# Three up projections of a fused transformer kernel: two-product wide form with halves added by VectorE, and a fourth low part made by GpSimd

## The reference, cut to what matters

```python
xt = x.reshape(T, D)                       # T = 256 tokens, D = 2048
q = (xt @ w_pq).reshape(T, PEER_HEADS, 2, PEER_HALF)
...                                        # top 16 of 128 x 128 keys for each of 8 heads, softmax gates
# the kernel computes, for all experts e in four quarters of 32 blocks of 128:
#   hid[e, t]  = gelu(u_emb[e] . x[t])           "up"
#   hid[e, t] *= gate[e, t]                      (gates spread from the chosen slots)
#   y[t]      += hid[e, t] * v_emb[e]            "down"
```

## Time and profile before

| what | value |
|---|---|
| time, median of 3 runs | 3218.45 us (3217.82 to 3219.81) |
| profiled execution | 3219.95 us, of it 3218.3 us span |
| PE busy | 3172.9 us, 99% |
| DVE busy | 2416.1 us, 75% |
| ACT busy | 1592.2 us, 49% |
| POOL busy | 644.3 us, 20% |
| chain that ended last | PE 88%, DVE 5%, issue 3%, ACT 2% |
| 256-column products of `block_product` | 3 lines x 2944 |
| low parts by DVE (L1985), mean | 872 x 1223 ns |
| low parts by POOL (L488), mean | 160 x 2439 ns |
| load of an `ada` tile, issue to landing | 4.6 us |

### The profile page before, as it was taken

One profiled execution on the slowest core, in us unless ns is written; L12 is line 12 of the kernel. 1 busy time (PEld: TensorE's weight loads), 2 busy tenths in 40 slices (PEclk: granted clock), 3 DMA queues, 4 the chain that ended last, 5 costly groups with the idle time before them and its releaser, 6 DMA issues.

```text
span 3218.3 us, 61750 instructions
## 1 busy us (share of the span) xinstructions
PE 3172.9 (99%) x20344; PEld 2833.6 (88%) x20344; DVE 2416.1 (75%) x3958; ACT 1592.2 (49%) x2291; POOL 644.3 (20%) x635
## 2 busy tenths in 40 slices
PE   8999999999999999999999999999999999999997
PEld 8898899999889998899878888888998888888886
DVE  6676577699778987799999776445899878655556
ACT  5764545433443345433444457655766444444443
POOL 1050058100111011100000115887221111100000
PEclk9999999999999999999999999999999999999999
DMA  6436555666887678866655884666776887866444
GB/s 214 147 109 190 182 165 182 194 212 213 255 265 219 213 222 258 267 198 213 200 179 175 269 265 146 189 191 205 243 235 206 293 274 232 257 194 190 146 137 157
DMA packets 185936, 667.80 MB, mean 208 GB/s; under 512 B 24192, under 2 KB 24416, under 8 KB 184528
## 3 DMA queue, kind: packets, MB, share of 16 engines
q1 hardware_dynamic: 149984, 545.91, 53.6%
q0 software_dynamic: 35824, 120.19, 12.2%
HBM read 663.82 MB, written 2.18 MB: 207 GB/s over the span
## 4 chain that ended last, share of the span: by engine, by line
PE 88%; DVE 5%; issue 3%; ACT 2%; POOL 1%; DMA 0%; DVEq 0%; ACTq 0%; POOLq 0%; SPq 0%
PE PS L577 11%; PE PS L579 11%; PE PS L578 11%; PE PS L591 8%; PE PS L1008 7%; PE PS L1010 7%; PE PS L1012 7%; PE PS L592 4%; PE PS L720 2%; PE PS L722 2%; PE PS L721 2%; PE PS L1194 2%; PE PS L1196 2%; PE PS L1198 2%; POOL w_lo L488 1%
## 5 line engine op out<-in xcount | busy, mean ns | idle before, releaser
L1372 ACT ACTIVATE w_hi<-raw 128x1024 fp32r<-128x1024 f32 x1032 | 1091.8, 1059 | 1330.5 <-PE PS L579 579.0
L1985 DVE TENSOR_TENSOR w_lo<-raw,w_hi 128x1024 fp32r<-128x1024 f32 x872 | 1065.5, 1223 | 501.5 <-ACT w_hi L1372 494.8
L577 PE MATMUL PS<-xt,w_hi 128*128 128x256 f32 x2944 | 849.5, 289 | 2.3 <-DVEq L2118 2.1
L578 PE MATMUL PS<-xt,w_hi 128*128 128x256 f32 x2944 | 833.3, 283 | 0.0
L579 PE MATMUL PS<-xt,w_lo 128*128 128x256 f32 x2944 | 833.1, 283 | 0.0
L577 PEld LDWEIGHTS PS<-xt,w_hi 128*128 128x128 f32 x2944 | 564.4, 192 | 10.9 <-issue 9.6
L591 PE MATMUL PS<-xt,w_hi 128*128 128x512 f32 x1560 | 563.9, 403 | 7.6 <-DVE xt L2040 4.2
L578 PEld LDWEIGHTS PS<-xt,w_hi 128*128 128x128 f32 x2944 | 565.0, 192 | 0.4
L579 PEld LDWEIGHTS PS<-xt,w_lo 128*128 128x128 f32 x2944 | 564.7, 192 | 0.0
L488 POOL TENSOR_TENSOR w_lo<-raw,w_hi 128x1024 fp32r<-128x1024 f32 x160 | 387.5, 2439 | 350.2 <-ACT w_hi L1372 222.4
L592 PE MATMUL PS<-xt,w_lo 128*128 128x256 f32 x1560 | 438.7, 281 | 0.0
(11 more groups left out here) (445 smaller groups left out, 4029.1 us busy)
## 6 DMA issues: line engine op xcount, KB each, us to landing
raw<-in_u_emb SPq DMA_DIRECT2D x256, 512.0 KB, 3.6
raw<-in_v_emb SPq DMA_DIRECT2D x256, 512.0 KB, 4.4
ada<-in_ada_w POOLq DMA_DIRECT2D x240, 256.0 KB, 4.6
raw<-in_xbc SPq DMA_DIRECT2D x96, 512.0 KB, 3.5
raw<-in_z SPq DMA_DIRECT2D x80, 512.0 KB, 3.6
raw<-in_q SPq DMA_DIRECT2D x64, 512.0 KB, 3.5
raw<-in_a_out SPq DMA_DIRECT2D x64, 512.0 KB, 4.3
raw<-in_k SPq DMA_DIRECT2D x48, 512.0 KB, 4.8
```

Source lines behind the costliest of these rows:

```text
L577: pe.matmul(o, w_h, x_h, start=start, stop=False, skip_group_check=True)
L578: pe.matmul(o, w_h, x_l, start=False, stop=False, skip_group_check=True)
L1372: act.activation(w_hi[:, u, :], raw[:, u, :], ACT.Copy).then_inc(hi_done, 1)
L1985: dve.tensor_tensor(w_lo[:, u, :], raw[:, u, :], w_hi[:, u, :].bitcast(F32), ALU.subtract)\
```

## The change

In up1, up2 and up3 a block is made by `wide_block`. ScalarE copies the second half of the bank to `second_half` (the buffer `xtmp`), VectorE adds both halves into `hid` (`halves_summed`), and ScalarE applies Gelu in place in `hid`. A block on TensorE waits for `halves_added` (the sum two blocks before) and not for the Gelu, but for the first body. In the loop GpSimd makes the low part of tile 3 of each body, after the three of VectorE; VectorE waits at the top of each body until all four of the body before are there.

```diff
-        WIDE = {"w_pq": 0, "xbc": 16, "k2": 64, "q2": 88}
+        WIDE = {"w_pq": 0, "up1": 16, "up2": 48, "up3": 80, "xbc": 112, "k2": 160, "q2": 184}
...
             for quarter in range(1, QUARTERS):
-                with pool.Fori(0, 16) as k:
+                f = FIRST_BODY[f"up{quarter}"]
+                with pool.Fori(0, 15) as k:
                     for slot, segment in enumerate((0, 5)):
                         ada_tile(f"up{quarter}", segment, k, quarter - 1, slot, ada)
+                    pool.wait_ge(lo_done, 4 * (k + (f + 1)) + 3)
+                    low(k + (f + 1), 3)
...
                         spread_parts(2 * j + b, n_before, b, 2 + 2 * b)
-                        pe.wait_ge(act_free, 2 * j + (ACT_BLOCKS[up] + b + 1))
-                        block_product(up, j, b, PS[:, b, 0:S])
+                        if type(j) is int:
+                            pe.wait_ge(act_free, ACT_BLOCKS[up] + b + 1)
+                        else:
+                            pe.wait_ge(sem("halves_added"), 2 * j + (WIDE[up] + b + 1))
+                        wide_block(up, j, b)
...
+                def half(i, b, body):
                     act.wait_ge(tile_used, 4 * body + 2 * b + 2)
-                    act.activation(one(hid[quarter % 2], i), PS[:, b, 0:S], ACT.Gelu_apprx_tanh).then_inc(act_free, 1)
+                    half_out(up, i, b).then_inc(sem("half_out"), 1)
+
+                def gelu(i):
+                    act.wait_ge(sem("halves_added"), i + (WIDE[up] + 3))
+                    act.activation(one(hid[quarter % 2], i), one(hid[quarter % 2], i), ACT.Gelu_apprx_tanh)\
+                        .then_inc(act_free, 1)
+
+                def body(j):
+                    high(j + (f + 1), 0)
+                    if type(j) is not int:
+                        gelu(2 * j - 1)
+                    high(j + (f + 1), 1)
+                    half(2 * j, 0, j + f)
+                    high(j + (f + 1), 2)
+                    gelu(2 * j)
+                    high(j + (f + 1), 3)
+                    half(2 * j + 1, 1, j + f)
...
                 for u in range(4):
                     stage_hid(quarter - 1, u, u)
+                gelu(30)
                 high(f + 16, 2)
                 high(f + 16, 3)
-                gelu(31, 1, f + 15)
+                half(31, 1, f + 15)
+                gelu(31)
...
+                def halves_summed(i, b):
+                    dve.wait_ge(sem("half_out"), i + (WIDE[up] + 1))
+                    dve.tensor_tensor(one(hid[quarter % 2], i), PS[:, b, 0:S], second_half[:, b, :], ALU.add)\
+                        .then_inc(sem("halves_added"), 1)
 
                 def body(j):
+                    dve.wait_ge(lo_done, 4 * (j + (f + 1)))
                     for u in range(4):
-                        low(j + (f + 1), u)
+                        if u < 3:
+                            low(j + (f + 1), u)
                         if u % 2 == 0:
                             key_rows(2 * j + (2 + u // 2), n_before, (quarter - 1) * EB, u // 2)
                             apply_parts(2 * j + u // 2, n_before, quarter - 1, u // 2, 2 + u // 2 * 2)
                         else:
                             ada_product(f"up{quarter}", j, u // 2, ada, acc_up)
+                            halves_summed(2 * j + u // 2, u // 2)
...
                 low(f + 16, 1)
+                halves_summed(30, 0)
                 dve.wait_ge(sem("gates_applied"), 2 + EB * quarter)
                 for u in range(4):
                     stage_hid(quarter - 1, u, u, u)
...
                 low(f + 16, 2)
                 low(f + 16, 3)
+                halves_summed(31, 1)
```

More of the change, by code:

```diff
@@ L519, in _ @@
             for quarter in range(1, QUARTERS):
-                with pool.Fori(0, 16) as k:
+                f = FIRST_BODY[f"up{quarter}"]
+                with pool.Fori(0, 15) as k:
                     for slot, segment in enumerate((0, 5)):
                         ada_tile(f"up{quarter}", segment, k, quarter - 1, slot, ada)
+                    pool.wait_ge(lo_done, 4 * (k + (f + 1)) + 3)
+                    low(k + (f + 1), 3)
+                for slot, segment in enumerate((0, 5)):
+                    ada_tile(f"up{quarter}", segment, 15, quarter - 1, slot, ada)
                 down = f"down{quarter - 1 if quarter < 3 else 3}"
@@ L1686, in up_stage @@
                 f = FIRST_BODY[f"up{quarter}"]
-                def gelu(i, b, body):
+                up = f"up{quarter}"
+                def half(i, b, body):
                     act.wait_ge(tile_used, 4 * body + 2 * b + 2)
-                    act.activation(one(hid[quarter % 2], i), PS[:, b, 0:S], ACT.Gelu_apprx_tanh).then_inc(act_free, 1)
[L1692 to L1698, removed]
+                    half_out(up, i, b).then_inc(sem("half_out"), 1)
[13 more added lines that the diff above has]
+                    half(2 * j + 1, 1, j + f)
+                body(0)
+                with act.Fori(1, 15) as j:
+                    body(j)
                 high(f + 16, 0)
+                gelu(29)
                 high(f + 16, 1)
-                gelu(30, 0, f + 15)
+                half(30, 0, f + 15)
                 act.wait_ge(sem("gates_applied"), 2 + EB * quarter)
@@ L2462, in up_stage @@
                 down = f"down{quarter - 1}"
+                up = f"up{quarter}"
                 link(dve.memset(acc_up[:, :, :], 0.0))
+                if quarter > 1:
+                    dve.wait_ge(stage_lo_done, CHUNKS[f"down{quarter - 2}"] + 2 * EB)
+                def halves_summed(i, b):
+                    dve.wait_ge(sem("half_out"), i + (WIDE[up] + 1))
+                    dve.tensor_tensor(one(hid[quarter % 2], i), PS[:, b, 0:S], second_half[:, b, :], ALU.add)\
+                        .then_inc(sem("halves_added"), 1)
                 def body(j):
+                    dve.wait_ge(lo_done, 4 * (j + (f + 1)))
                     for u in range(4):
-                        low(j + (f + 1), u)
+                        if u < 3:
+                            low(j + (f + 1), u)
                         if u % 2 == 0:
@@ L2480, in up_stage @@
                     body(j)
+                dve.wait_ge(lo_done, 4 * (f + 16))
                 low(f + 16, 0)
```

## The result

| | before | after |
|---|---|---|
| time, median of 20 runs | 3217.75 us (3215.25 to 3222.06) | 3226.89 us (3222.59 to 3230.74) |
| profiled execution | 3219.95 us, span 3218.3 | 3226.84 us, span 3224.9 |
| DVE busy | 2416.1 us | 2439.0 us |
| POOL busy | 644.3 us | 758.0 us |

The ratio is 1.0026, 95% interval 1.002 to 1.0032: slower by 9 us. I had forecast slower, but by 59 us: 3278, with a range from 3236.

What follows compares the result with a forecast made beforehand. TensorE bounds the kernel, with VectorE nearly full; the change makes VectorE the bound. Loops +50.9 and tails +8.5 sum to +59.4 us: 3279.4 against its own execution, forecast as 3278, range 3236 to 3302.

Steps and rivals of the forecast that it cites:

- Step 1, TensorE's products: Up loops: two wide products instead of three narrow save 0.095 us a block, 9.2 us at most; TensorE needs 12.16 a body.
- Step 2, VectorE's steps: Up loops: one low part leaves, two sums of halves come; VectorE's own steps fill 11.36 us a body, below TensorE's 12.16.
- Step 3, the stall: Up loops: GpSimd's low part locks out VectorE's `hot_gate`, 2.15 us a body; body 13.51 us, loops together +50.9 us.
- S + 7.9: Up loop body: GpSimd asks about 7.9 us after VectorE's body start S, during `hot`, and gets in behind it.
- rival A (the short stall): Up loops: GpSimd starts only with the sum of gates, `hid` waits 1.2 us; body 12.6, 3238 us; chance 0.16.
- Step 4, the tails: Ends of up1 to up3: VectorE's tail precedes the last Gelu; +1.9, +1.9 and +4.7 us, together +8.5.
- rival D: Up loops: TensorE's idle of 1.3 us a body halves its clock for microseconds in many bodies; +20, 3299 us; chance 0.06.

Runs made afterwards that it cites:

- runs 13 and 14: After with narrow last blocks and the last Gelu ahead of ScalarE's last high part: with GpSimd's low part 3209.08 us, without it 3207.57 us.
- run 7: After plus an extra VectorE write of 128 x 256 in each loop body: 3279.16 us.
- Runs 6 and 8: After plus a 128x512 VectorE write a body: without GpSimd's low part 3247.48 us; with it waiting for the last `hot_gate` 3269.06 us.
- Run 4: After plus products that nobody reads in TensorE's waits for the last Gelu at the stage ends: 3221.46 us.
- run 3: After with the last block of each up stage in the narrow form, Gelu straight from `PS`: 3211.16 us.
- run 11: After plus two VectorE writes (128 x 768 and 128 x 512) once per stage, behind the third body: 3234.65 us.
- run 12: After plus an extra VectorE write of 128 x 64 in each loop body: 3258.23 us.
- run 5: After plus an extra VectorE write of 128 x 512 in each loop body, GpSimd's low part kept: 3294.07 us.
- run 2: The kernel before, narrow products kept, with only GpSimd making each body's fourth low part: 3218.86 us.
- run 9: After plus one VectorE write of 128 x 768 per stage behind the third body, GpSimd's low part kept: 3228.54 us.

## Why the prediction was wrong

The term that failed is VectorE's own steps, 11.36 us a body where 11.09 were measured. With it fell the conclusion that VectorE comes late and loses 2.15 us a body to GpSimd: it lost 1.1 us, and TensorE stayed the bound.

**Step 1, TensorE's products: right.** The body that TensorE can do is 12.18 us (I had 12.16), and without the tails the whole gain shows (runs 13 and 14).

**Step 2, VectorE's steps: the term that was mis-sized.** I had 11.36 us, it is 11.09. I took 0.74 for `ada_product` from a distance of 1.05 us less 0.31 of waiting, but an instruction that waits loses its overlap with the one before: from start to start it is 0.66 (641.47 to 642.13), and 0.08 twice a body is most of the error. The prediction's own tail had it right: 1.32 for two, from a stretch in which VectorE didn't wait. The sum of halves is 0.33 and not 0.38, which is another 0.10 for two.

**Step 3, the stall: the lock was right, but GpSimd came in at another place.** 11.09 + 1.1 us is just TensorE's 12.18, so VectorE stays nearly on time. ScalarE's high part of tile 3 then follows TensorE, and GpSimd asks at S + 8.6 (638.87 - 630.28), late in the three `hot_gate`, instead of S + 7.9. In run 7, as in the prediction, it follows the Gelu and with it VectorE's halves (ScalarE's timelines, after and then run 7):

```profile
637.72 1.06 ACT L1380 ACTIVATE w_hi<-raw 128x1024 fp32r<-128x1024 f32 x1 [0.71 <-PE PS L599]
```
```profile
650.08 0.42 ACT L1705 ACTIVATE hid<-hid  x1 [1.96 <-DVE hid L2496]
650.40 1.04 ACT L1381 ACTIVATE w_hi<-raw 128x1024 fp32r<-128x1024 f32 x1
```

Run 7 puts 0.20 of the missing 0.27 us back, and the long stall comes, with 3279 us. Runs 6 and 8 show that it isn't the write as such: the larger write costs 20 us without GpSimd, and with GpSimd moved the long stall stays away. So 0.20 us in a body of 12 were worth some 52 us in the whole. I had given rival A (the short stall) a body of 12.6 us, from the same 11.36; with the right steps its mechanism is what happened, but the body stays at TensorE's pace.

After itself is near that edge. VectorE is slower than TensorE by 0.01 to 0.02 us a body: from the second body of up1 to the last the request slips from 0.55 to 0.32 us behind the first `hot_gate`, in up3 to 0.24, and GpSimd still comes in behind all three each time.

The Trainium skill (SBUF — State Buffer, section Who interferes with whom) says that whoever issues first gets the pair for the whole instruction. The runs agree, with `hid` at 1.52 us and three `hot_gate` at 2.90. What decided here is between which of several queued instructions the other engine gets in.

**Step 4, the tails: right as waits, but short of their price.** Waits of 3.06, 3.13 and 5.96 us stand where I had put them. Together the tails are 1.8 + 1.8 + 4.6 = 8.2 us longer (forecast 8.5). What I left out is the clock. In rival D I had priced it for short idles in the loops, which didn't come, and not for the longest waits of the change. Run 4 gives 5.4 us for it, and run 3, without waits and what follows them, 15.7: the 10.6 us of waits and the 5.4 are 16.0, which is the whole within the spread of the runs. The waits of 0.52 us in run 3 have no such stretch behind them.

**The sum as measured.** Loops -2.0, -0.5 and -0.3 us by the windows (the last two have one stretch at half clock more in them than before, 1.7 us each), tails +8.2: +5.4. The spans differ by 6.6; of the 1.2 us left, the clock's record gives +6.8 for four stretches of 3.4 us behind the ends of up1 to up3, and -3.4 for two fewer in later stages; -2.2 us are not assigned.

**What stays open.** Which gap of VectorE's lets GpSimd in. A request 0.28 us ahead of `hot_gate` got in before it in one body of run 11, and one at 0.27 on either side did not; a request 0.35 us behind it got in at once in run 12, while requests at 0.34 in after waited 0.21 us and came in behind all three. If the distance decides, then by about 0.01 us, and not by one threshold. In run 5 a request 0.55 us ahead of `hot_gate` got in before it, while in run 2 one as far ahead waited 3.50 - 2.40 = 1.10 us and came in behind all three (GpSimd's and VectorE's timelines of run 2, first body of up2):

```profile
1003.59 3.50 POOL L488 TENSOR_TENSOR w_lo<-raw,w_hi 128x1024 fp32r<-128x1024 f32 x1 [12.68 <-DVE w_lo L1990]
```
```profile
1004.14 0.69 DVE L2434 TENSOR_TENSOR hot_gate<-hot,slot_gate 128x256 bf16<-128x256 bf16 x3
```

No run isolates what else counts. Also, a half-clock stretch at 1004 us in after, 8 us into VectorE's loop of up2, has no long wait ahead of it and is not explained. Run 3, which has no long waits at all at the stage ends, has it too, at 1002 us; it is gone in runs 4, 13 and 14. The kernel before has one at 1380 us, in up3.

## What to carry to other kernels

When two engines that lock each other out are both near full, compute the body for both outcomes of each collision and compare each with the bottleneck's pace; if the pace lies between, the error of the sum of steps decides, and the forecast should be two-sided instead of one likeliest case. Take steps from start to start only where the instruction behind did not wait. Where a change adds a wait of microseconds to TensorE, add the half-clock stretch behind it (here 1.7 us behind a wait of 3 us, 3.4 us behind one of 6), and look first whether the last block of a stage can keep the form with the shorter chain to the next stage.

## What the runs showed of the hardware

A VectorE instruction with two SBUF operands and a GpSimd subtraction of 128 x 1024 exclude each other at bf16 as at float32: three `hot_gate` (bf16) went from 0.69 to 2.90 us. The sum of gates, which reads `PS`, kept its 0.95 us while GpSimd ran (638.93 beside 638.87). GpSimd, too, waited: in run 11 its 2.39 us are stretched to 3.23. And the loss is not smooth: 0.02 us of work a body was worth 31 us (run 12), and a write of 0.7 us once per stage nothing that shows (run 9, 3228.5 against 3226.9 us).
